# Norms around the expert stage: a norm by columns with products led ahead of it, and GpSimd adding seven of eight tiles for five sums

## The reference

```python
def first_block(x, c, ctx, ...):
    mod_x = silu(c) @ w_mod + b_mod ...                 # six modulation vectors
    # neighbourhood attention and a gated linear recurrence
    x = x + gt1 * (concatenate([na_x, hg_x]) @ w_out)
    # second norm, then the experts
    x = x + gt2 * peer_ffn(modulate(rms_norm(x, norm2), sh2, sc2), peer_wq, peer_keys, peer_u, peer_v)
    return rms_norm(x, norm_f)

def peer_ffn(...):      # per token: 8 heads x 16 experts out of 16384
    q = t @ wq; s = q . sub_keys; top, idx = ...top_k...; g = softmax(top)
    a = gelu(u[idx] . t)
    return sum_k (g * a)_k * v[idx]_k                   # 128 expert rows per token

def second_block(x, ...):
    for l in range(2):
        m = even_mixer(x, ...) if l % 2 == 0 else odd_mixer(x, ...)
        x = layer_norm(ALPHA * x + m, ln1_g[l], ln1_b[l])
        f = conv_ffn(x, ...)
        x = layer_norm(ALPHA * x + f, ln2_g[l], ln2_b[l])
```

## Time and profile before

| | us |
|---|---|
| median of three runs | 3481.75 |
| the profiled execution | 3480.46 |
| its span, first to last instruction | 3478.6 |
| PE busy | 2803.8 (81%) |
| PEld busy | 2315.0 (67%) |
| DVE busy | 2065.8 (59%) |
| ACT busy | 1220.8 (35%) |
| POOL busy | 757.9 (22%) |
| mean granted TensorE clock | 0.891 |

### The profile page before, as it was taken

One profiled execution on the slowest core, in us unless ns is written; L12 is line 12 of the kernel. 1 busy time (PEld: TensorE's weight loads), 2 busy tenths in 40 slices (PEclk: granted clock), 3 DMA queues, 4 the chain that ended last, 5 costly groups with the idle time before them and its releaser, 6 DMA issues. The chain is left out here.

```text
span 3478.6 us, 38862 instructions
## 1 busy us (share of the span) xinstructions
PE 2803.8 (81%) x14536; PEld 2315.0 (67%) x14536; DVE 2065.8 (59%) x3696; ACT 1220.8 (35%) x2184; POOL 757.9 (22%) x694
## 2 busy tenths in 40 slices
PE   6999888995556655565555689889999999899998
PEld 5887677784545545554555567667888777778886
DVE  3224775577776855784444455446874465668743
ACT  2112433245555555555555541242120103421201
POOL 0002452024444444444444411000000000100000
PEclk9999999997777777677777789989999999999999
DMA  6999998779999999999999942202232231023322
GB/s 220 320 285 289 309 300 271 237 282 384 421 421 421 421 421 421 418 420 421 418 421 420 421 160 91 67 19 73 97 96 91 73 116 54 19 73 96 96 91 73
DMA packets 155057, 848.12 MB, mean 244 GB/s; under 512 B 15440, under 2 KB 15696, under 8 KB 88208
## 3 DMA queue, kind: packets, MB, share of 16 engines
q0 software_dynamic: 82624, 575.97, 41.0%
q1 hardware_dynamic: 72272, 269.99, 24.6%
HBM read 841.70 MB, written 136.31 MB: 281 GB/s over the span
## 5 line engine op out<-in xcount | busy, mean ns | idle before, releaser
L206 PE MATMUL PS<-AR_r,RHI 128*128 128x512 f32 x1888 | 751.4, 398 | 27.0 <-DVE RING_r L1536 8.5
L864 PE MATMUL PS<-IDN,HL 128*128 128x128 f32 x2688 | 497.0, 358 | 342.4 <-ACT HL L1366 342.4
L208 PE MATMUL PS<-AR_r,RING_r 128*128 128x512 f32 x1888 | 737.5, 391 | 0.0
L864 PEld LDWEIGHTS PS<-IDN,HL 128*128 128x128 f32 x2688 | 429.9, 187 | 408.5 <-ACT HL L1366 404.9
L1742 DVE SCALAR_TENSOR_TENSOR AR<-AR 128x1024 f32<-128x1024 f32 x378 | 462.6, 1225 | 347.9 <-DMA AR<-peer_uv,XC 347.4
L207 PE MATMUL PS<-AR_r,RHI 128*128 128x512 f32 x1504 | 586.1, 390 | 0.0
L526 POOL DMA_INDIRECT AR<-peer_uv,XC x378 | 429.1, 1135 | 585.3 <-ACT HL L1366 290.3
L1534 DVE CAST RHI<-RING 128x1024 fp32r<-128x1024 f32 x256 | 178.1, 696 | 458.1 <-DMA RING<-in_wstream 450.2
L206 PEld LDWEIGHTS PS<-AR_r,RHI 128*128 128x128 f32 x1888 | 356.2, 189 | 111.8 <-issue 23.7
L208 PEld LDWEIGHTS PS<-AR_r,RING_r 128*128 128x128 f32 x1888 | 356.0, 189 | 74.9
L864 PE MATMUL PS<-IDN,AR 128*128 128x128 f32 x1408 | 260.5, 358 | 172.4 <-ACT AR L1366 172.4
(11 more groups left out here) (355 smaller groups left out, 3715.6 us busy)
## 6 DMA issues: line engine op xcount, KB each, us to landing
RING<-in_wstream SPq DMA_DIRECT2D x304, 512.0 KB, 3.5
peer_uv<-in_peer_u SPq DMA_DIRECT2D x50, 1024.0 KB, 16.1
peer_uv<-in_peer_v SPq DMA_DIRECT2D x50, 1024.0 KB, 16.9
peer_uv<-in_peer_u POOLq DMA_DIRECT2D x14, 1024.0 KB, 22.0
peer_uv<-in_peer_v POOLq DMA_DIRECT2D x14, 1024.0 KB, 23.0
AR<-peer_uv,XC POOLq DMA_INDIRECT x378, 14.8
XL<-in_xl SPq DMA_DIRECT2D x1, 2048.0 KB, 8.0
AR<-in_strips POOLq DMA_DIRECT2D x1, 2048.0 KB, 8.7
```

The source lines that it names most:

```text
L206: pe.matmul(out, sh, mh, start=start, stop=False)
L208: return pe.matmul(out, sl, mh, start=False, stop=stop)
L864: mm = pe.matmul(sum_bank(tt, k), scaled_row(n)[:, P * k:P * k + P], IDN[:], start=(j == 0 and k % 4 == 0), stop=(j == SLOTS - 1), is_tran ...
```

## The change

The code does six things.

1. Six of the eight sum matmuls of the second norm and of the four means are replaced. GpSimd adds the first seven tiles (of squares, or of XL) one after another into STAT, `add_seven`; TensorE does two matmuls, one on STAT and one on the eighth tile, `with_seven`. The variances are left as they are.
2. GpSimd passes barrier 7 behind these adds, ahead of its last four copies, and does not wait there.
3. The early slots begin one chunk earlier (EARLY_FROM 5), and 20 are taken inside wq. EXP_AT becomes [0, 4, 16, 36, 94, 184, 312]: the exponentials of parts 1 and 2 stand at slots 4 and 16, both inside wq. VectorE's order is moved to match: dots from its chunk 9 on, best_pairs(1) behind chunk 10's split.
4. The norm nf is done in two column groups, tokens 0 to 383 (the first three token tiles) and 384 to 511. The first group is done amid the 128 slots of the last token tile, at fixed slots (ADD_AT, SQUARE_AT, SUM_AT, ROOT_AT, SCALE_AT, LEAD_AT = 24, 40, 56, 64, 72, 96 behind the tile's first slot). Gain and scaling are one VectorE instruction.
5. The three led chunks of rq are split by VectorE there, too, and their products with the first 384 columns are done in eight portions at slots 96 to 103 of that tile (`lead_rq(0, k)`); those with the last 128 columns follow behind the second group (`lead_rq(1, k)`). The rows that lay over RHI lie elsewhere in the last tile (LATE_ROWS), the slots' sums use banks 3, 4, 5 and 7, and the split input X2S and the tables DECAY and the masks have other places.
6. Barriers 8 and 9 go, and the later ones are numbered anew.

```diff
-EXP_AT = [0, 0, 18, 36, 94, 184, 312]
-EARLY, EARLY_IN_WQ, EARLY_FROM = 24, 18, 6
+EXP_AT = [0, 4, 16, 36, 94, 184, 312]
+EARLY, EARLY_IN_WQ, EARLY_FROM = 24, 20, 5
+LAST = SLOTS * (TT - 1)
+NORM_COLS = (slice(0, LAST // SLOTS * P), slice(LAST // SLOTS * P, S))
+ADD_AT, SQUARE_AT, SUM_AT, ROOT_AT, SCALE_AT, LEAD_AT = (LAST + a for a in (24, 40, 56, 64, 72, 96))
...
# GpSimd
+            def add_seven(s, ready, x):
+
+                for k in range(KT - 1):
+                    after(pool, s, ready, k + 1, KT)
+                    if k >= 2:
+                        steps.wait()
+                    if k >= 1:
+                        ins = pool.tensor_tensor(STAT[:], STAT[:] if k >= 2 else x[:, 0, :], x[:, k, :], ALU.add)
+                        if k < KT - 2:
+                            steps.done(ins)
+                ins.then_inc(seven_added, 1)
...
             pool.dma_start(KEYS, t["keys"]).then_inc(s_keys, 16)
+            add_seven(n2, "sq", SQUARES)
+            passing(pool, 7)
             pool.wait_ge(chunk_used, FIRST["out"] + KT)
             for i in late:
                 copy_rows(pool, i, uv_copied_late)
-            barrier(pool, 7)
...
-            barrier(pool, 8)
-
+            pool.wait_ge(scaled_used, SLOTS * TT)
...
+            add_seven(ln[0], "res", XL)        # and so for ln[1], ln[2], ln[3]
...
# TensorE
+            def with_seven(n, x, s, ready, total):
+
+                def last(k):
+                    if k < KT - 1:
+                        return
+                    pe.wait_ge(seven_added, n)
+                    pe.matmul(bank(6), ONES[:], STAT[:], start=True, stop=False)
+                    after(pe, s, ready, KT, KT)
+                    pe.matmul(bank(6), ONES[:], x[:, k, :], start=False, stop=True).then_inc(s[total], 1)
+
+                return last
...
             for n in range(EARLY_IN_WQ, SLOTS * TT):
                 if n % SLOTS == 0 and n >= 2 * SLOTS:
                     pe.wait_ge(tile_added, n // SLOTS - 1)
                 add_slot(n)
-            barrier(pe, 8)
-
+                if n == SUM_AT:
+                    norm_sum(0)
+                if n == LEAD_AT:
+                    pe.wait_ge(w_split, nth_split(FIRST["rq"] + 2) + 1)
+                if LEAD_AT <= n < LEAD_AT + KT:
+                    lead_rq(0, n - LEAD_AT)
+            keep_clock(5, 6)
+            norm_sum(1)
+            keep_clock(5, 4)
             for k in range(KT):
-                rms(nf)(k)
-            passing(pe, 9)
-            keep_clock(5, 13)
+                lead_rq(1, k)
...
# ScalarE
             def scale_pair(n):
+                if n in EXP_AT[1:]:
+                    top_exp(EXP_AT.index(n))
...
             for n in range(EARLY_IN_WQ, SLOTS * TT, 2):
-                if n in EXP_AT:
-                    top_exp(EXP_AT.index(n))
+                if n == SQUARE_AT:
+                    norm_square(0)
+                if n == ROOT_AT:
+                    norm_root(0)
                 scale_pair(n)
-            barrier(act, 8)
-
-            rms(nf, lambda k: par("norm_f")[:, k:k + 1], lambda k: 0.0, XL)
-            barrier(act, 9)
+            act.preload_act_table_set(LN_EXP)
+            norm_square(1)
+            norm_root(1)
...
# VectorE, in wq
+                if c == 9:
+                    dve.wait_ge(ht_evac, 2 * TT)
+                dots_to(2 * (c - 8))
+                split_chunk(FIRST["wq"] + c)
                 if c == 10:
-                    dve.wait_ge(ht_evac, 2 * TT)
-                dots_to(2 * (c - 9))
-                split_chunk(FIRST["wq"] + c)
-                if c == 8:
                     best_pairs(1, nothing)
...
-            dots_to(14)
-            best_pairs(2, up_to(16))
+            dots_to(16)
+            best_pairs(2, nothing)
+            dots_to(20)
             first_keys(0, range(11, 16), up_to(22))
...
# VectorE, behind token tile 2
-            add_tile(TT - 2, whole_tile)
-            barrier(dve, 8)
-
-            add_tile(TT - 1, lambda k, ins: ins.then_inc(nf["res"], 1))
-            first_chunks("rq")
-            normed(nf, "x2", XL, X2S)
-            barrier(dve, 9)
+            dots_to(ADD_AT)
+            add_tile(TT - 2, norm_tile)
+            dve.wait_ge(row_scaled, LAST)
+            for c in range(ahead):
+                split_chunk(FIRST["rq"] + c)
+                dots(3)
+            dots_to(SCALE_AT)
+            scale_and_split(0, dots)
+            dots_to(SLOTS * TT)
+            add_tile(TT - 1, norm_tile)
+            scale_and_split(1, nothing)
```

More of the change, by code:

```diff
@@ L403, in row @@
         def row(n):
-            return EARLY_ROWS[n % NEARLY] if n < EARLY else ROWS_UV[n % NROW]
+            if n < EARLY:
+                return EARLY_ROWS[n % NEARLY]
+            return LATE_ROWS[n % NROW - 6] if n >= LAST and n % NROW >= 6 else ROWS_UV[n % NROW]
         def row_signal(n):
@@ L566, in tile, with tiles @@
                 return [x[:, k, cols] for x in xs]
-            def tiles(c, n, xs, name, to, free, base=0, xs2=None, to2=None, follow=None, lead=None, lag=2):
+            def tiles(c, n, xs, name, to, free, base=0, xs2=None, to2=None, follow=None, lead=None, lag=2, led=False):
                 together = 3 if base == 0 else 0
-                if together:
+                if together and not led:
                     pe.wait_ge(w_split, nth_split(c + together - 1) + 1)
-                for k in range(KT if together else 0):
+                for k in range(KT if together and not led else 0):
                     if lead is not None:
@@ L637, in add_up @@
                     mm.then_inc(s[total], 1)
+            def with_seven(n, x, s, ready, total):
[7 more added lines that the diff above has]
+                return last
             def rms(s):
[L640 removed]
+                return with_seven(1, SQUARES, s, "sq", "sum")
             def mean(s):
[L643 removed]
+                return with_seven(2 + s["use"], XL, s, "res", "mean")
             def variance(s):
                 for k in range(KT):
[L647 removed]
+                    add_up(7, SQUARES, k, s, "sq", "sum")
             def modulation(c, which, b):
@@ L867, in add_slot, with norm_sum, lead_rq @@
                 mm.then_inc(scaled_used, 1)
+            def norm_sum(g):
+                for k in range(KT):
+                    after(pe, nf, "sq", KT * g + k + 1, KT)
+                    mm = pe.matmul(bank(6)[:, NORM_COLS[g]], ONES[:], norm_squares(g, k), start=(k == 0),
+                                   stop=(k == KT - 1), skip_group_check=True)
+                mm.then_inc(nf["sum"], 1)
+            def lead_rq(g, k):
+                split("x2", KT * g + k)
+                for i in range(3):
+                    mm = three_passes(bank(i)[:, NORM_COLS[g]], parts(FIRST["rq"] + i, k), tile(X2S, k, NORM_COLS[g]), pe,
+                                      k == 0, k == KT - 1)
+                    if g == 1 and k == KT - 1:
+                        mm.then_inc(chunk_used, 1)
             tiles(FIRST["wq"], 16, H2S, "h2", main, wq_evac, follow=key_scores, lag=1)
@@ L884, in _ @@
             for name in ("rq", "rk", "rg", "sq", "sk"):
-                b = tiles(FIRST[name], 4, X2S, "x2", main, free, b)
+                b = tiles(FIRST[name], 4, X2S, "x2", main, free, b, led=name == "rq")
             for name, first in (("rv", 4), ("sv", 0)):
```

113 lines of the change are left out of this document (71 added, 42 removed).

## The result

The changed kernel takes 3445.31 us (median of 4 runs, 3438.76 to 3449.12), the kernel before 3480.97 in the same session: ratio 0.9888, 95% interval 0.9876 to 0.9901. A second session gave 0.9896 (0.9880 to 0.9913). So 35.7 us were gained where 48 were forecast. The profiled execution took 3447.99 us, its span is 3446.2.

The account below looks back on a forecast made before the run. DMA engines bound the expert stage, TensorE the dense projections and ffn. Savings of 21.1 + 9 + 0 + 18.0 = 48.1 us from 3480.46 gave 3432.4, 3433.7 on the median's footing, forecast 3433; 8 in 10 for 3421 to 3449.

Parts of the forecast that it names:

- R1: Rival: second norm and early slots give nothing, the stream's start stays at 798; 3441 us, chance 0.18.
- part B: Second norm, barrier 7, early slots: gather 24 goes at 789 instead of 798.2, stream's end moves by 9 us (2 to 16).
- the signs that I had named: Checks in the changed profile on sums, wq waits, DMA share, tail and stream's end, some with limits that would refute.
- second sign: End of the expert stream: the forecast falls if it moves by under 3 us.
- A: Four layer means: six fewer TensorE matmuls each, 5.28 us apiece in dense stages, sum 21.1 us (15 to 22).
- C: Work moved under the last token tile (tile 3): hidden beside DMA-bound rows, cost 0; if uncovered, 5 to 10 us.
- R3: Rival, bubbles: led products at the lower clock make the gathers stand, stream loses 8 to 10 us; 3442, chance 0.10.
- R5: Rival: VectorE or TensorE sets tile 3's pace for all 128 rows; 3497 at 0.5 us a row, chance 0.02.
- D: Tail after the last dot, on 128 columns: 36.0 us becomes 18.0, gain 18.0 (11 to 20).
- R4: Rival, short products: the tail stays at the lower clock, 7 to 8 us lost; 3441, chance 0.08.

Follow-up runs that it names:

- e7: Changed kernel with the dots of rows 4, 5 and 16, 17 between the steps of VectorE's expert choices instead of behind them; ratio to the kernel before 0.9882.
- e5: Changed kernel with TensorE doing all eight sums of the second norm and GpSimd at barrier 7 behind its copies, as before; 3450.45 us, ratio 0.9914.
- e12: The changed kernel itself, without any edit, traced and measured again; ratio to the kernel before 0.9896.
- e8: Changed kernel with four of SyncE's table copies moved to GpSimd's last ones, all held until VectorE has split the third wq chunk; ratio 0.9897.
- e2: Changed kernel with GpSimd's last four table copies held until VectorE has split the third wq chunk; 3445.84 us, ratio 0.9902.
- e9: Changed kernel with e7's edit, 34 instead of 22 identity matmuls behind the second norm's sum, e2's wait, two SyncE copies moved to GpSimd; 3436.53 us, ratio 0.9855.
- e10: Kernel of e9 with six unread identity matmuls behind each of the last twelve pairs of slots; ratio to the kernel before 0.9861.

## Why the prediction was right and wrong

The time, 3445.3, lies in the range and 12 us above the forecast; it lies in the range because that was drawn wide enough to hold R1. The step that failed is part B's result, "The stream is DMA bound from there, so its end moves by 9 us": gather 24 did not move (O + 183.50 for 183.54). The case that came is R1, by a longer way than R1 told. Of the signs that I had named two came: TensorE's waits in wq are 1.08 + 3.20 + 4.18 = 8.5 us (part B wrong above 6), and the stream's end moved by under 3 us, from 2028.38 to 2029.24. By that second sign the forecast fell, whatever the time says.

*A, forecast 21.1:* 20.8 in the trace, 19.5 alone, 21.0 on average. No wait for GpSimd ahead of the two sums. Of the 0.2 to 0.3 us that three of the means lack of 5.28, 0.2 lie at the burst: one sum fewer gave 0.68 us there (4.19 to 3.51) instead of 0.88. The Trainium skill (GPSIMD Engine Reference, Key points) states contention with GpSimd for VectorE instructions with two SBUF inputs. The trace agrees: beside the adds VectorE's split subtraction took 2.20 us instead of 1.22, and the residual that reads PSUM 0.67 as ever. The adds themselves took up to 1.67 instead of 1.29. It stayed in VectorE's slack.

*B, forecast 9, measured 0.* The bill, from O to the last key scores, is +11.0 where I had +2: the first product +1.8 (forecast 1.5); the led products at half clock +2.3, since TensorE stood 7.2 us, which I did not ask about; slots 0, 1 come 5.2 cheaper (forecast 3.4 in wait; the rest is clock); two more slots +1.9 as forecast; slots 4, 5 +4.6, which I missed: I noted that best_pairs(1) no longer stands ahead of the first dots, and not whose dots it stands ahead of now; slots 16, 17 +5.7 (forecast 2 to 4), for VectorE's choice and not for the exponential, as e7 and the ScalarE rows show. These sum to 11.1. That the 12 us between the last scores and gather 24 would go was right: 13.8 became 2.7. The landing at the edge was right too, and its holder wrong. With eight sums the split starts at O + 37.8 to 37.9, with no wait for the chunk to speak of (it landed at O + 36.1 in e5 and at 37.9 in the kernel before). With GpSimd's sum the chunk is issued 3 us earlier, but VectorE waits for it, and the split starts at O + 37.6 to 40.4 in the seven traces that keep SyncE's copies, at 33.7 to 34.3 in the three that move them. So the 3.9 us taken from TensorE (forecast 4.4) became idle time, and idle time cost the clock.

*C, forecast 0:* 1230.4 beside 1230.2 us from gather 24 to the last dot, with a DMA share of 1.01 up to 2021. R3 and R5 did not come.

*D, forecast 18.0 with 11 as the end at 1.2 GHz:* 18.3 in five traces, 9.5 to 12.1 in four. In e12 the led products start 9.2 us behind the last dot's end (forecast 9.0) and end 17.3 behind it (forecast 18.0, of which 1.1 was for the clock). The mechanism and the size were right for these. What the sum lacked is that the same code comes with or without a fall of the clock, so that R4 is true in about half of the traces (mean gain of the nine 14.8). In the first trace the led products end 23.9 us behind the last dot's end. The 72 led products of e12 run from 2037.84 to 2045.9, 112 ns each, and VectorE needs 0.85 us a tile where TensorE needs 1.01. The estimate from the rows (0.11) holds, and VectorE doesn't bind. The Trainium skill (TensorE: Matmul & The Clock Gate, Back-to-back issue gap) gives about 81 ns for a matmul of 128 columns in a stream; this case measured 112. The prediction's 6.3 us for VectorE's splits doesn't follow from its 0.75 us a tile, which is 6.0 for eight; at 0.85 they are 6.8.

With 21.0 + 0 + 14.8 = 35.8 the sum meets the 35.7 that were measured. That it meets them so closely is luck: A and D are means over different kernels, B differs by 1 us between the changed kernel's two traces, and its two tails by 8.

## What to carry to other kernels

Work taken off an engine ahead of a transfer that is already late turns into idle time, and on TensorE idle time may be paid twice, by the clock of what follows (here 7.2 us idle and 2.3 us in the led products): fill the wait, and move the transfer's rivals before the arithmetic. When steps are reordered ask for each moved block which queued item it now stands ahead of, on its own engine; the wait may be shown at another one. Take more than one trace, and count from landmarks, before a stage's gain is believed.

## What the hardware showed that I had not expected

- TensorE's granted clock fell to 0.50 at 2044, within work that had run without a gap since 2041.26, and stayed there until 2057.5 though TensorE was busy 6.00 of 6 us, and in another execution of the same kernel that stretch ran at 1.0.
- A weight chunk of 512 KB landed in 3.5 us with the copies of 1 MB around it moved away (e8), and in 13.7 to 16.6 with SyncE's in its queue, whether GpSimd's were held back (e2) or not (e7).
- Code that no edit touches reaches the same place up to 12.5 us apart (O at 611.4 to 623.9); e9 and e10, which differ only in the tail, have 623.9 and 613.6.
- Matmuls of 128 columns in fp32r, each with a weight load, ran at 112 ns at full clock and 213 at half.
